# Six chunks of the second block's modulation: from the rotary stage on TensorE to the state-space output stage on VectorE

## What is computed

```python
# first block
mod = jax.nn.silu(c) @ ada_w + ada_b                  # 1024 x 3072
shift, scale, gate = jnp.split(mod, 3, axis=-1)
h = rms_norm(x, norm_g) * (1.0 + scale) + shift
proj = h @ w_in                                       # q, k, v, z_att, indexer, z_ssm, xbc, dt, gates
o_att = sparse_attention(...) * jax.nn.silu(z_att)
y_ssm = ssd(...)                                      # normed and gated, then @ w_branch_ssm
merged = jax.nn.sigmoid(g_att) * (o_att @ w_branch_att) + jax.nn.sigmoid(g_ssm) * y_ssm
x = x + gate * (merged @ w_out)
# second block
mod2 = jax.nn.silu(c_2) @ w_ada_2 + b_ada_2           # 1024 x 6144: shift1 scale1 gate1 shift2 scale2 gate2
h = rms_norm_2(x, norm1_gain) * (1.0 + scale1) + shift1
x = x + gate1 * mix(h)                                # band attention and a gated delta rule
h2 = rms_norm_2(x, norm2_gain) * (1.0 + scale2) + shift2
return x + gate2 * peer(h2)                           # product-key experts
```

## Time and profile before

| | us |
|---|---|
| median of 3 timed runs | 3002.66 (3001.50 to 3003.53) |
| the profiled execution, its own time | 2994.11 |
| its span, first to last instruction | 2992.30 |
| busy: PE, DVE, POOL, ACT | 2625.3, 1659.1, 1169.9, 795.6 |
| rotary stage | 158.7 to 243.5 |
| selection stage | 243.5 to 333.0 |
| state-space output stage | 860.5 to 1086.0 |

### The profile page before, as it was taken

The page is one execution under the profiler, slowest core; times in us unless marked ns, Lnnn a source line. Parts: engine busy times, 40 slices in busy tenths (PEclk is TensorE's granted clock), DMA queues, the critical chain, the costliest instruction groups (busy, mean ns, idle before and its releaser), DMA issues.

```text
span 2992.3 us, 26054 instructions
## 1 busy us (share of the span) xinstructions
PE 2625.3 (88%) x8398; PEld 1372.6 (46%) x8398; DVE 1659.1 (55%) x3647; ACT 795.6 (27%) x1616; POOL 1169.9 (39%) x1091
## 2 busy tenths in 40 slices
PE   7999899999979979989799899979877778767777
PEld 3444444445544436467675465546422223223232
DVE  2056823345510124364379998765677777777764
ACT  2013312138730012232234323221312112212121
POOL 0000000013310000000057777656777777777776
PEclk8999999999989989999899899989999899989999
DMA  7226103122221113321379989999999999999998
GB/s 307 74 113 274 64 30 112 57 85 71 65 91 56 57 64 133 127 85 57 109 257 357 354 305 379 380 351 344 357 376 395 400 408 405 405 405 405 406 402 354
DMA packets 185462, 709.01 MB, mean 237 GB/s; under 512 B 20416, under 2 KB 43344, under 8 KB 175216
## 3 DMA queue, kind: packets, MB, share of 16 engines
q0 software_dynamic: 147456, 536.94, 46.7%
q1 hardware_dynamic: 37584, 169.45, 15.2%
q10 hardware_dynamic: 288, 0.96, 0.1%
HBM read 703.01 MB, written 4.27 MB: 236 GB/s over the span
## 4 chain that ended last, share of the span: by engine, by line
PE 22%; POOL 14%; issue 7%; DMA 5%; DVE 3%; ACT 0%; POOLq 0%; SPq 0%; DVEq 0%; ACTq 0%
PE bank L3193 14%; POOL ring L3001 11%; PE bank L488 4%; DMA ring<-in_peer_expert_down,experts 3%; POOL second_arena L3001 3%; DVE ring L3076 1%; PE bank L2035 0%; DMA second_arena<-in_peer_expert_down,experts 0%; DMA ring<-in_peer_expert_up,experts 0%; DMA x_rows_scratch<-second_arena 0%; DMA out<-xT 0%; PE bank L2012 0%; PE bank L2329 0%; PE bank L2336 0%; PE bank L2334 0%
## 5 line engine op out<-in xcount | busy, mean ns | idle before, releaser
L3193 PE MATMUL bank<-ring,xT 128*128 128x512 f32 x1516 | 765.6, 643 | 189.0 <-ACT xT L3169 81.4
L3076 DVE CUSTOM_DVE_ANT_0 ring<-ring,second_arena 128x1024 f32<-128x1024 f32 x380 | 465.9, 1226 | 219.8 <-DMA ring<-in_peer_expert_down,experts 172.4
L3193 PEld LDWEIGHTS bank<-ring,xT 128*128 128x128 f32 x1516 | 292.2, 203 | 600.4 <-issue 376.3
L3001 POOL DMA_INDIRECT ring<-in_peer_expert_up,experts x384 | 412.5, 1074 | 159.0 <-issue 96.7
L3001 POOL DMA_INDIRECT ring<-in_peer_expert_down,experts x380 | 402.4, 1059 | 131.3 <-issue 114.3
L488 PE MATMUL bank<-hT,ring 128*128 128x512 f32 (+2 forms) x1168 | 433.2, 530 | 6.4 <-DMA ring<-in_weights 1.8
L488 PEld LDWEIGHTS bank<-hT,ring 128*128 128x128 f32 (+1 forms) x1168 | 222.3, 193 | 211.0 <-issue 199.8
L1420 POOL TENSOR_TENSOR xs_skip<-xs_rows,rows 128x512 f32<-128x512 f32 x16 | 24.7, 1546 | 727.4 <-ACT xs_rows L1298 638.3
L3001 POOL DMA_INDIRECT second_arena<-in_peer_expert_down,experts x132 | 137.0, 1038 | 434.9 <-DVE experts L3059 390.6
L3169 ACT ACTIVATE xT<-consts,expert_coefs 128x128 f32<-128x128 f32 x505 | 177.9, 394 | 414.4 <-PE bank L3193 278.5
L3193 PE MATMUL bank<-second_arena,xT 128*128 128x512 f32 x504 | 239.2, 607 | 22.5 <-DMA second_arena<-in_peer_expert_up,experts 22.4
(11 more groups left out here) (527 smaller groups left out, 3107.7 us busy)
## 6 DMA issues: line engine op xcount, KB each, us to landing
ring<-in_weights SPq DMA_DIRECT2D x65, 2048.0 KB, 8.1
second_arena<-in_weights SPq DMA_DIRECT2D x12, 1024.0 KB, 8.2
decay<-acum_scratch SPq DMA_DIRECT2D x16, 512.0 KB, 5.2
ring<-in_peer_expert_up,experts POOLq DMA_INDIRECT x384, 7.3
ring<-in_peer_expert_down,experts POOLq DMA_INDIRECT x380, 7.1
second_arena<-in_peer_expert_down,experts POOLq DMA_INDIRECT x132, 6.5
x_rows<-in_x SPq DMA_DIRECT2D x1, 2048.0 KB, 12.0
x_rows_scratch<-second_arena SPq DMA_DIRECT2D x2, 1024.0 KB, 8.7
```

Of the source, the lines that this page charges most:

```text
L3001: pool.indirect_dma_start(out=slot[seat[n]], out_offset=None, in_=d[f"peer_expert_{kind}_2"], in_offset=bass.IndirectOffsetOnAxis(ap=exper ...
L3076: post(dve, dve.tensor_tensor_reduce(row, row, h_row(i), 1.0, 0.0, ALU.mult, ALU.add, dots[:, u % 2, s:s + 1]), dotted)
L3193: last = pe.matmul(k.bank[half][:], diag[n % DR], row[:, half * 512:(half + 1) * 512], start=(h == 0 and s == 0), stop=(h == RH - 1 and s ...
```

## The change

The second block's chunks 0 to 5 (columns 0 to 23 of `mod2`) leave the rotary stage with all that belonged to them: 48 products in strips, six turns, twelve copies on ACT, and their six places in the ring. z's two chunks now follow each other. In the ring the six chunks stand in the state-space output stage: one behind each gate chunk, one behind each pair of the branch, one behind each chunk of `w_out`.

There, for each of them, DVE (`mod_sums`) multiplies the chunk's eight blocks of 128 x 512 by the eight per-partition scalars of `silu_c` and adds them up: one `tensor_scalar` and seven `scalar_tensor_tensor` on SBUF, each waited for, into one of two buffers. PE (`mod_columns`) adds over the partitions: four products with a 128 x 128 piece of the sum as the weight and a single column of ones, into four columns of bank 7, and counts the chunk as used. The stage's projection therefore has seven banks instead of eight. DVE makes three of the sums before its first merge, the fourth after four merges, the fifth before w_out's evictions, the sixth after four of these. At the end it adds the bias from bank 7 into `mod2`. Selection adds the bias to the other 24 columns only.

```diff
 def weight_order():
-    out += za[0:1] + ada[0:2] + za[1:2] + ada[2:6]
+    out += za
     out += ada[6:8] + ga[0:1] + ada[8:10] + ga[1:2] + ada[10:12]
...
-    out += cut("w_in", GS0, 1024)
-    for c in (0, 512):
-        out += cut("w_branch_ssm", c, 512) + cut("w_branch_ssm", c, 512, D)
-    out += cut("w_out", 0, 1024)
+    gs, wo = cut("w_in", GS0, 1024), cut("w_out", 0, 1024)
+    out += gs[0:1] + ada[0:1] + gs[1:2] + ada[1:2]
+    for i, c in enumerate((0, 512)):
+        out += cut("w_branch_ssm", c, 512) + cut("w_branch_ssm", c, 512, D) + ada[2 + i:3 + i]
+    out += wo[0:1] + ada[4:5] + wo[1:2] + ada[5:6]
...
 def attention_rotary_stage(k, t):
-            k.stream(sp, m.steps[steps[-1]][2])
+            k.stream(sp, plan[-1][1][-1])
...
-            silu_z(range(3, 4))
-            m.on_scalar(act, steps[:2])
-            silu_z(range(4, 8))
-            m.on_scalar(act, steps[2:3])
+            silu_z(range(3, 8))
...
-            m.on_scalar(act, steps[3:])
...
-            pj.run(pe, slice(0, 1))
-            m.on_tensor(pe, steps[:2])
-            pj.run(pe, slice(1, 2))
-            m.on_tensor(pe, steps[2:3])
+            pj.run(pe)
...
-            m.on_tensor(pe, steps[3:])
...
 def ssm_out_stage(k, t):
-        pj = Projection(k, ctx, "ssm_out", plan)
+        pj = Projection(k, ctx, "ssm_out", plan, banks=range(7))
...
+            def mod_columns(n):
+                pe.wait_ge(sums_in.sem, n + 1)
+                for b in range(4):
+                    at = 4 * n + b
+                    last = pe.matmul(k.bank[7][:, at:at + 1], sums[:, n % 2, b * P:(b + 1) * P], k.const("ones", 1),
+                                     start=True, stop=True)
+                last.then_inc(k.used.sem, 1)
+                k.used.n += 1
+
+            for n in range(n_branch):
+                pj.run(pe, slice(n, n + 1))
+                mod_columns(n)
             pe.wait_ge(merged.sem, 8)
-            pj.run(pe, slice(n_branch, None))
+            for n in range(n_branch, n_branch + 2):
+                pj.run(pe, slice(n, n + 1))
+                mod_columns(n)
...
+            def mod_sums(n):
+                g = m.later[n]
+                w = k.take(dve, g)
+                if n > 1:
+
+                    dve.wait_ge(k.used.sem, m.later[n - 2] + 1)
+                out = sums[:, n % 2, :]
+                post(dve, dve.tensor_scalar(out, w[:, 0, :], m.silu_c[:, 1, 0:1], None, ALU.mult), k.vstep)
+                for kk in range(1, KD):
+                    ins = dve.scalar_tensor_tensor(out, w[:, kk, :], m.silu_c[:, 1, kk:kk + 1], out, ALU.mult, ALU.add)
+                    post(dve, ins, sums_in if kk == KD - 1 else k.vstep)
+
+            mod_sums(0)
+            mod_sums(1)
+            mod_sums(2)
             dve.wait_ge(pj.freed.sem, 8)
             for j in range(8):
+                if j == 4:
+                    mod_sums(3)
...
+            mod_sums(4)
             for j in range(8):
+                if j == 4:
+                    mod_sums(5)
...
+            dve.wait_ge(k.used.sem, m.later[-1] + 1)
+            made = 4 * len(m.later)
+            post(dve, dve.tensor_tensor(k.mod2[:, 0:made], k.bank[7][:, 0:made], k.col("b_ada_2", 0, made), ALU.add), k.vstep)
```

More of the change, by code:

```diff
@@ L182, in __init__ @@
         self.silu_c = k.keep("silu_c", [P, 2, 8])
-        self.gs = [find(k, "ada_w", 0, 3072), find(k, "w_ada_2", 0, 6144)]
-        self.steps = [(which, i, g) for which in range(2) for i, g in enumerate(self.gs[which])]
-        self.alone = len(self.gs[0]) + len(self.gs[1]) // 2
+        self.gs = [find(k, "ada_w", 0, 3072), find(k, "w_ada_2", 3072, 3072)]
+        self.later = find(k, "w_ada_2", 0, 3072)
+        self.steps = [(0, i, g) for i, g in enumerate(self.gs[0])]
+        self.steps += [(1, i + len(self.later), g) for i, g in enumerate(self.gs[1])]
+        self.alone = len(self.gs[0])
         self.row_in = k.ctx.enter_context(k.nc.semaphore("mod_row_copied"))
@@ L584, in attention_rotary_stage @@
         pj = Projection(k, ctx, "attention_z", plan, banks=range(5))
[L585 to L588, removed]
         pos_in = ctx.enter_context(nc.semaphore("positions_loaded"))
@@ L733, in selection_stage @@
         m.rows_buffer(ctx, "mod2_rows_b")
-        first = len(m.gs[0]) + len(m.gs[1]) // 2
+        first = len(m.gs[0])
         steps = [range(first + 2 * i, first + 2 * i + 2) for i in range(3)]
@@ L834, in _ @@
             dve.wait_ge(m.columns_in, len(m.steps))
-            v(dve.tensor_tensor(k.mod2[:], k.mod2[:], k.col("b_ada_2", 0, 48), ALU.add))
+            late = slice(4 * len(m.later), 48)
+            v(dve.tensor_tensor(k.mod2[:, late], k.mod2[:, late], k.col("b_ada_2", 24, 24), ALU.add))
             dve.wait_ge(spread, 1)
@@ L1458, in ssm_out_stage @@
         plan += columns(find(k, "w_out", 0, 1024), k.merged)
-        pj = Projection(k, ctx, "ssm_out", plan)
+        pj = Projection(k, ctx, "ssm_out", plan, banks=range(7))
         merged = Signal(ctx, nc, "branches_merged")
+        m = k.modulation
+        sums = ctx.enter_context(nc.sbuf_tensor("mod2_sums", [P, 2, 512], F32))
+        sums_in = Signal(ctx, nc, "mod2_sums_ready")
         block = ctx.enter_context(nc.Block())
@@ L1464, in _ @@
         def _(sp):
-            k.stream(sp, plan[-1][1][-1])
+            k.stream(sp, k.modulation.later[-1])
         @block.tensor
         def _(pe):
-            pj.run(pe, slice(0, n_branch))
+            def mod_columns(n):
[9 more added lines that the diff above has]
+                mod_columns(n)
             pe.wait_ge(merged.sem, 8)
-            pj.run(pe, slice(n_branch, None))
+            for n in range(n_branch, n_branch + 2):
+                pj.run(pe, slice(n, n + 1))
+                mod_columns(n)
         @block.scalar
```

## The result

| | before | after |
|---|---|---|
| median of the timed runs, us | 3002.08 (3000.13 to 3003.53, 4 runs) | 2970.69 (2963.73 to 2975.96, 4 runs) |
| span of the profiled execution | 2992.30 | 2961.7 |
| ratio, 95% interval | | 0.9898 (0.9872 to 0.9924) |

The account below looks back on a forecast made before the run. PE was taken to bound the kernel, stage gains passing on whole: 19.7 + 0.9 - 4.4 = 16.2 us less, giving 2977.9 profiled and 2986.5 for the median. Range 2980 to 2995.

Parts of the forecast that it names:

- What bounds the kernel now: Whole kernel: PE, busy 88% of the span, bounds rotary and state-space output stages; what a stage wins is passed on whole.
- First two steps: Rotary stage, modulation steps between the z chunks: z then runs unbroken, ending at 213.96 instead of 224.38; 10.4 us less.
- third: Rotary stage, modulation step between z and the first transpose: only the wait for ACT's last silu remains; 2.8 us less.
- last three: Rotary stage, final modulation steps: in the changed kernel ACT's last copy of turned rows ends the stage; 6.5 us less.
- Loads moved: Selection's start: second step's chunk lands earlier, removing PE's 0.87 us wait; 0.9 us less, bounds 0 to 3.5.
- Added on PE: Output stage: six one-column groups, four at 0.98 us, one hidden at the merge, last 0.5; 4.4 us more, bounds 3.5 to 7.
- Added on DVE: Output stage: sums of 6.0 us per chunk, 36 us in all, hidden; the tightest has some 13 us to spare.
- A: Output stage: one-column groups let the clock fall, 2.4 us after each of five exposed groups; 12 us, 2998.5; chance 0.07.
- B: Output stage: clock falls lastingly after the one-column groups; at 10 us each 25 us more, 3011, slower; chance 0.03.
- C of the prediction: Output stage: PE waits for DVE's sums, each taking 24 us; 9 us together, 2995.6; chance 0.04.
- D: Ahead of attention: low z clock, late gate chunk or ACT returns part of the gain; 5 us at most, 2991.5; chance 0.08.
- After the stage: Behind the output stage: second block's chunks load later but in time, ACT's removed copies save no table load; nothing changes.

## Why the prediction was wrong, and what of it was right

**What bounds the kernel now**: right. PE's 19.5 us in the rotary stage arrived at attention undiminished.

**First two steps, 10.4 us; third, 2.8; last three, 6.5; sum 19.7**: right, 19.5 (13.2 for the first two terms, 6.3 for the last). z took 55.17 us against 55.20; transposes came at 215.29 and selection at 224.63, against 214.7 and 223.9, in a run whose z began 0.5 us later. DVE did not become the bound.

**Loads moved, 0.9 us less**: misread. The wait stayed, 0.86 us; ACT's copy took the load's place, which was the lower bound, and the row at 286.81 above shows that the kernel before has this wait without any load. Selection is 0.6 us shorter all the same, by where PE's low clock falls. The first L208 group takes 3.64 us, nearly twice the 1.92 of the second, with a granted clock of 0.50; in the kernel before the low clock takes in selection's first product, the first L205 group in part (2.55 us), and a part of the first gate chunk (28.47 us against 27.73). After, then before, columns as in the earlier trace rows:

```profile
226.60:230.30 3.70, 3.67 (x18) 0.59 (x16) 3.45 (x8) 0.82 (x3) 0.00 (x0) 0.50 0.93 399
235.30:264.50 29.20, 29.20 (x75) 12.80 (x74) 27.33 (x75) 5.21 (x9) 0.00 (x0) 1.00 0.23 97
```

```profile
243.50:245.60 2.10, 2.01 (x9) 1.27 (x9) 1.38 (x2) 0.75 (x2) 0.00 (x0) 0.50 1.02 437
253.20:284.00 30.80, 30.80 (x73) 13.34 (x73) 28.83 (x80) 5.21 (x9) 0.00 (x0) 0.94 0.30 127
```

That this comes out at 0.6, near the 0.9, is luck. The gate chunk was in time.

**Added on PE, 4.4 us more**: 3.7. A group takes 0.95 us and puts the next product 0.81 us off, where the row chosen (L217) said 1.05 and 0.98. The cover at the merge was there as said.

**Added on DVE, 6.0 us a chunk, hidden**: 0.49 + 5.47 us, and gaps of 0.03. With S = 841.11 the second chunk was taken at S+37.5 (35.7 predicted) and the later ones at S+71.0, 126.7, 177.7 and 207.0 (74, 131, 178 and 208 predicted), so each is summed 14 us or more before PE asks.

**Rivals.** A and B did not come: the output stage has a granted clock of 0.99, and no chunk after a group is long. (The clock of 1.00 around the merge wait, which the prediction put against A, stands in no row that it named; the window from 1026 to 1034 us of the kernel before does show it.) The rule of the Trainium skill, page "TensorE: Matmul & The Clock Gate", section "HAM oscillation — how this bites in real kernels", that pauses between bursts bring the low clock back, did not show behind groups of 0.95 us; behind the pauses of 4.92 and 3.60 us (the fourfold sums) the granted clock is 0.76 and 0.82 and the streams are 2.3 and 1.7 us longer, on the rule's side. C of the prediction, PE waiting for the sums, needed four times DVE's work to appear. D didn't come.

**The step that failed** is the first paragraph's last clause together with "I put the difference of the two kernels on the median unchanged": that what the stages win is passed on whole, and nothing else. With it falls the paragraph "After the stage", which puts everything behind the output stage at nothing and looks only at weight loads and ACT's copies. The win is passed on whole, 16.3 us; but 14.8 us more went behind the output stage: 3.0 in norm, 3.2 in the second block up to its late queries, 8.6 in the expert phase. I had taken norm and the 1882 us of the second block as one fixed length, read from one execution. It is not fixed: the kernel before lies between 2988 and 3021 us in 40 runs on two chips with the full-rate stream. Part of the 14.8 us behind the output stage is such variation: the norm's product L397 took 10.16 us in the profile of before, in the stretch with a clock of 0.65, and L400 takes 7.13, and that stage comes out at 19.8 to 22.9 us over the profiles of either kind. The larger part, 11 to 18 us beyond the 16.3 with the padding taken off, repeats in six sets of runs on such chips, and by the profiles its place is the expert phase, whose stream has longer slow stretches in the kernel before. What in the changed kernel spares it these isn't settled: start times and output stage length were excluded, the place of code loads was not, and on the chips with the slower stream the two sets of the changed kernel leave 2 ± 4 and 7 ± 7 us beyond the 16.3. So the cause of this part stays open. The range had no term for any of this; one for the difference between executions, some 10 us to both sides, would just have held the result, but by luck: the surplus repeats, so it isn't such a difference.

## What to carry to other kernels

Six steps on the bound engine cost about the same wherever they stand (19.5 us in one stage, 22.5 in the other); it pays to give the bulk to an engine that idles and leave the bound one only what it alone can do, here 0.81 us a chunk. Cost an edit in its own stages, where each term held within 1 us, but give the stages behind it a term of their own when they are bound by a stream: profile several executions for the length of that phase before calling a difference of 0.5% yours. Before you read a wait as a load's, see whether the same wait stands elsewhere without one. And a filler experiment tells something only on a chip where the effect is seen, so measure the unchanged pair beside it on the same chip.

## What the runs showed of the hardware

The same gather stream ran at 403 to 409 GB/s on the chips where the kernel before takes 3002 us, and at 351 to 371 where it takes 3093 to 3106 (windows of 200 us). Most of the difference lies in the expert phase: 867 against 957 us in profiles of the kernel before. On the first kind of chip stretches of 20 to 200 us fall to 360 to 390. The Trainium skill, page "DMA: Bandwidth & Descriptors", section "Bandwidth", gives one core alone up to about 425 GB/s and each of two cores that stream from one memory domain roughly 358. The upper level seen lies 4 to 5% under the first figure, the lower one around the second; whether another core was streaming, no run here shows.

Executions of one kernel on one chip differ with a standard deviation of 3 to 9 us, as much as half of what this edit wins in its own stages; six or twelve runs against 17 to 35 bring the difference of the means to ± 4 to 7 us.
